# An encoder's bidirectional recurrence on one core: the identity of the last two doubling levels added by GpSimd, and the inputs of the carried states multiplied 128 wide

## The reference

```
def _rwkv7_step(S, inp):
    r, w, k, v, a, b = inp
    Sa = jnp.einsum('zbhvk,zbhk->zbhv', S, a)
    S = S * w[..., None, :] + Sa[..., :, None] * b[..., None, :] + v[..., :, None] * k[..., None, :]
    return S, jnp.einsum('zbhvk,zbhk->zbhv', S, r)
...
    xs = (shared(r), per_dir(decay), per_dir(kd), shared(v), -kk_s, kk_s * per_dir(a))
    S0 = jnp.zeros((2, B, H, N, N), f32)
    _, ys = lax.scan(_rwkv7_step, S0, xs)
    y = jnp.moveaxis(ys[:, 0] + jnp.flip(ys[:, 1], axis=0), 0, 1)
```

## Time and profile before

| | us |
|---|---|
| median of 3 runs | 1809.4 (1805.44 to 1811.64) |
| the profiled execution's own time | 1806.69 |
| its span in the profile | 1804.9 |
| recurrence, eight passes | 368.9 to 590.0 of the span |
| TensorE busy | 1709.2 (95%) |
| VectorE busy | 556.7 (31%) |
| ScalarE busy | 334.5 (19%) |
| GpSimd busy | 71.3 (4%) |

### The profile page before, as it was taken

The page is one execution under the profiler, slowest core; times in us unless marked ns, Lnnn a source line. Parts: engine busy times, 40 slices in busy tenths (PEclk is TensorE's granted clock), DMA queues, the critical chain, the costliest instruction groups (busy, mean ns, idle before and its releaser), DMA issues.

```text
span 1804.9 us, 36910 instructions
## 1 busy us (share of the span) xinstructions
PE 1709.2 (95%) x15975; PEld 1092.5 (61%) x15975; DVE 556.7 (31%) x1270; ACT 334.5 (19%) x966; POOL 71.3 (4%) x114
## 2 busy tenths in 40 slices
PE   8999999989999999999999999999999999999996
PEld 7887888877777445576554545454444444454543
DVE  2001333577875101023123232222223222322233
ACT  2122222156656101022100000000000000000002
POOL 1000000010100000002000000000000000000000
PEclk9999999999999999999999999999999999999998
DMA  9932344200000925247999999999999999999994
GB/s 303 216 112 97 117 136 171 93 4 4 4 4 5 366 100 193 105 175 269 398 388 427 433 425 434 427 434 428 432 429 431 428 432 428 432 430 426 413 423 191
DMA packets 100784, 503.61 MB, mean 279 GB/s; under 512 B 38204, under 2 KB 42704, under 8 KB 81472
## 3 DMA queue, kind: packets, MB, share of 16 engines
q1 hardware_dynamic: 95960, 489.22, 67.7%
q0 software_dynamic: 4464, 12.03, 2.3%
q10 hardware_dynamic: 248, 0.65, 0.1%
HBM read 511.29 MB, written 4.23 MB: 286 GB/s over the span
## 4 chain that ended last, share of the span: by engine, by line
PE 73%; DMA 20%; DVE 4%; issue 2%; SPq 1%; ACT 1%; POOL 0%; DVEq 0%; ACTq 0%; PEldq 0%
PE ps L1598 15%; DMA ring<-in_wd 9%; PE ps L2120 9%; DMA ring<-in_wu 9%; PE ps L2112 8%; PE ps L2263 8%; PE ps L1930 6%; PE ps L2128 4%; PE ps L1813 2%; PE ps L1948 2%; PE ps L1999 2%; PE ps L2016 2%; PE ps L1957 2%; DMA ring<-in_wg 1%; PE ps L1816 1%
## 5 line engine op out<-in xcount | busy, mean ns | idle before, releaser
L1598 PE MATMUL ps<-wide,ring 128*128 128x256 f32 x1248 | 275.3, 379 | 1.2 <-PE ps L1598 0.9
L1598 PEld LDWEIGHTS ps<-wide,ring 128*128 128x128 f32 x1248 | 239.0, 195 | 39.7 <-issue 10.1
L2120 PE MATMUL ps<-ring,wide 128*64 128x256 f32 x1472 | 172.0, 394 | 24.1 <-DMA ring<-in_wu 24.1
L1458 DVE TENSOR_TENSOR tokA<-tokA,ps 128x512 f32<-128x512 f32 x256 | 158.5, 681 | 105.0 <-PE ps L2128 105.0
L2112 PE MATMUL ps<-ring,wide 128*64 128x256 f32 x1600 | 180.5, 383 | 4.4 <-DMA ring<-in_wg 2.4
L2263 PE MATMUL ps<-ring,gg 128*64 128x512 f32 x736 | 168.1, 598 | 2.8 <-DMA ring<-in_wd 2.8
L2120 PEld LDWEIGHTS ps<-ring,wide 128*64 128x64 f32 x1472 | 109.6, 142 | 84.8 <-DMA ring<-in_wu 28.5
L1471 DVE SCALAR_TENSOR_TENSOR gg<-ps,tmp,gg 128x256 f32<-128x256 f32 x32 | 15.5, 484 | 471.0 <-PE ps L2120 471.0
L2112 PEld LDWEIGHTS ps<-ring,wide 128*64 128x64 f32 x1600 | 114.4, 138 | 62.6 <-issue 4.3
L2128 PE MATMUL ps<-wide,gg 64*128 64x512 f32 x512 | 135.3, 627 | 0.6 <-ACT wide L889 0.6
L2263 PEld LDWEIGHTS ps<-ring,gg 128*64 128x64 f32 x736 | 48.7, 136 | 116.8 <-issue 106.1
(11 more groups left out here) (361 smaller groups left out, 1994.8 us busy)
## 6 DMA issues: line engine op xcount, KB each, us to landing
ring<-in_wu SPq DMA_DIRECT2D x20, 4096.0 KB, 29.0
ring<-in_wg SPq DMA_DIRECT2D x19, 4096.0 KB, 29.6
ring<-in_wd SPq DMA_DIRECT2D x19, 4096.0 KB, 30.4
rest<-in_wd SPq DMA_DIRECT2D x8, 4096.0 KB
ring<-in_w_in SPq DMA_DIRECT2D x7, 4096.0 KB, 15.9
rest<-in_wg SPq DMA_DIRECT2D x6, 4096.0 KB
rest<-in_wu SPq DMA_DIRECT2D x6, 4096.0 KB
ring<-in_w_out SPq DMA_DIRECT2D x4, 4096.0 KB, 17.6
```

Of the source, the lines that this page charges most:

```text
L1458: V.tensor_tensor(fin_part(t, h, n), fin_part(t, h, n), ps[:, banks[q][h], :], ALU.add).then_inc(S["added"], 1)
L1598: ins = mm(ps[0:rows_, m % 2, 0:T], lhs, hnT[:, k, :], start=k == 0, stop=k == KD - 1)
L2120: ins = mm(ps[CAP * h:CAP * h + CAP, 1, 0:T], xT[:, k, CAP * i:CAP * i + CAP], w[:, T * h:T * h + T], start=k == 0, stop=k == KD - 1)
```

## The change

In levels 4 and 5 the identity is added to the power by GpSimd, into a new tile `PI`, so that one product (P + I)·R takes the place of P·R + R. The step then waits for GpSimd and no longer for ScalarE directly. `rw_r1` and `rw_ks` become one counter `rw_plus`, which GpSimd raises 14 times in a pass. The input products of the states are taken for both heads at once: 64 rows of weights, 128 columns, 128 wide moving data. The two off-diagonal blocks of the result are not used. `SS` becomes 128 wide, and ScalarE copies 128 columns in place of 64.

```
-        SS = late[:, 5120:5376].rearrange("p (z i n) -> p z i n", z=2, i=2)
+        PI = late[:, 5888:6400].rearrange("p (g e n) -> p g e n", g=4, e=2)
+        SS = late[:, 5120:5632].rearrange("p (z i n) -> p z i n", z=2, i=2)
...
             for n in range(4 * CT):
                 pool.wait_ge(S["rw_mask"], n + 1)
-                pool.tensor_tensor(PRN[1][:, n % 4, :, 1, :], GB[:, n % 4, :, 0, :], eye, ALU.add).then_inc(S["rw_r1"], 1)
+                pool.tensor_tensor(PRN[1][:, n % 4, :, 1, :], GB[:, n % 4, :, 0, :], eye, ALU.add).then_inc(S["rw_plus"], 1)
                 if n % 4 == 3:
                     for b in range(TB):
-                        pool.tensor_tensor(KS[:, b], GK[:, b, :, 1, :], GK[:, 2 + b, :, 1, :], ALU.add).then_inc(S["rw_ks"], 1)
+                        pool.tensor_tensor(KS[:, b], GK[:, b, :, 1, :], GK[:, 2 + b, :, 1, :], ALU.add).then_inc(S["rw_plus"], 1)
+                    for i in range(8):
+                        pool.wait_ge(S["rw_pte"], 23 * (n // 4) + 12 + i)
+                        pool.tensor_tensor(PI[:, i % 4], PRN[i // 4][:, i % 4, :, 2, :], eye, ALU.add).then_inc(S["rw_plus"], 1)
...
-                        A(SS[:, z, i % 2, :], ps[:, S_BANK[i % 2] + 2 * z, T:T + CH], ACT.Copy).then_inc(S["rw_se"], 1)
+                        A(SS[:, z, i % 2, :], ps[:, S_BANK[i % 2] + 2 * z, T:T + P], ACT.Copy).then_inc(S["rw_se"], 1)
...
                     if n == 11:
                         pe.wait_ge(S["rw_pv"], p + 1)
+                    elif l >= 4:
+                        pe.wait_ge(S["rw_plus"], 14 * p + 6 + n - 15)
                     else:
                         pe.wait_ge(S["rw_pte"], 23 * p + (n - 3 if n < 11 else n - 4))
...
-                    lo = 0 if l < 4 else 1
-                    for e, r, q, o in tiles():
-                        mm(ps[o, 2 * g + e, CH * lo:P], src[q, g, e, 2, :], src[q, g, e, lo:2, :].rearrange("p k n -> p (k n)"),
-                           start=True, stop=False)
-                    for e, r, q, o in tiles():
-                        ins = mm(ps[o, 2 * g + e, CH:P], ident[q, q], src[q, g, e, 1, :], start=False, stop=True)
+                    if l < 4:
+                        for e, r, q, o in tiles():
+                            mm(ps[o, 2 * g + e, 0:P], src[q, g, e, 2, :], src[q, g, e, 0:2, :].rearrange("p k n -> p (k n)"),
+                               start=True, stop=False)
+                        for e, r, q, o in tiles():
+                            ins = mm(ps[o, 2 * g + e, CH:P], ident[q, q], src[q, g, e, 1, :], start=False, stop=True)
+                    else:
+                        for e, r, q, o in tiles():
+                            ins = mm(ps[o, 2 * g + e, CH:P], PI[q, g, e, :], src[q, g, e, 1, :], start=True, stop=True)
...
-                        for e in range(2):
-                            mm(ps[half_of(e), S_BANK[i % 2] + 2 * z, T:T + CH], NB[q, g, P + CH * e:P + CH * e + CH], X[q, g, 0, e, :],
-                               start=True, stop=False)
-                        for e in range(2):
-                            ins = mm(ps[half_of(e), S_BANK[i % 2] + 2 * z, T:T + CH], NB[q, g, T + CH * e:T + CH * e + CH], value(q, g % 2, e),
-                                     start=False, stop=i == 0)
+                        heads = ps[:, S_BANK[i % 2] + 2 * z, T:T + P]
+                        mm(heads, NB[q, g, P:T], X[q, g, 0].rearrange("p e n -> p (e n)"), start=True, stop=False)
+                        ins = mm(heads, NB[q, g, T:T + P], Vtok[q, g % 2, P * p:P * p + P], start=False, stop=i == 0)
```

More of the change, by code:

```diff
@@ L271, in encoder @@
         ya_tr ya_ev rw_sq rw_n2 rw_bonus_in rw_bon rw_q rw_exp rw_prep rw_n2e rw_y0e rw_gram rw_mask rw_gnow rw_v0 rw_sums rw_pv rw_kv rw_x0
-        rw_x0ev rw_pt rw_pte rw_rh rw_tte rw_r1 rw_xf rw_xe rw_ks rw_y0 rw_s rw_se rw_ys rw_yp
+        rw_x0ev rw_pt rw_pte rw_rh rw_tte rw_plus rw_xf rw_xe rw_y0 rw_s rw_se rw_ys rw_yp
         rw_mu rw_dsq rw_var rw_out op_mm op_add xk_mm xk_ev xs_mm xs_max xs_exp xs_p xs_tr xs_trev xo_mm xo_ev
@@ L1855, in pair_ @@
                                 mm(ps[half_of(e), 2 * b + h, T:T + CH], X[q, g, 0, e, :], GB[q, g, e, 1, :], start=z == 0, stop=False)
-                    pe.wait_ge(S["rw_ks"], 2 * p + b + 1)
+                    pe.wait_ge(S["rw_plus"], 14 * p + 4 + b + 1)
                     for h in range(2):
@@ L1886, in carried @@
                         q = half_of(e)
-                        ins = mm(ps[q, S_BANK[i % 2] + 2 * z, T:T + CH], TT[q, g, :], SS[q, z, (i - 1) % 2, :], start=False, stop=True)
+                        n = slice(CH * e, CH * e + CH)
+                        ins = mm(ps[q, S_BANK[i % 2] + 2 * z, T + CH * e:T + CH * e + CH], TT[q, g, :], SS[q, z, (i - 1) % 2, n], start=False, stop=True)
                     ins.then_inc(S["rw_s"], 1)
@@ L1893, in outputs @@
                         q = half_of(e)
-                        ins = mm(ps[q, 5 + 2 * z, T + CH * c:T + CH * c + CH], SS[q, z, i % 2, :], RH[q, g, CH * h:CH * h + CH],
+                        ins = mm(ps[q, 5 + 2 * z, T + CH * c:T + CH * c + CH], SS[q, z, i % 2, CH * e:CH * e + CH], RH[q, g, CH * h:CH * h + CH],
                                  start=True, stop=True)
```

2 lines of the change are left out of this document (1 added, 1 removed).

## The result

| | changed kernel | kernel before |
|---|---|---|
| median, us | 1809.4 (1805.35 to 1814.97, 20 runs) | 1806.54 (1803.29 to 1811.64, 20 runs) |
| ratio, 95% interval | 1.0016 [1.0009, 1.0023] | |
| profiled execution: own time, span | 1809.79, 1808.0 | 1806.69, 1804.9 |

Both columns come from the same chip, in turns. The change costs 2.9 us, 0.16%: no change by the bound of 0.3%, but more than nothing by the interval. The two profiled executions are 3.1 us apart.

The account below looks back on a forecast made before the run. TensorE was taken to bound the doubling levels, with some idle waits for instructions. Terms -0.93 + 1.40 - 0.75 + 0.67 gave +0.39 us a pass, 3.1 in eight; forecast 1812 us, range 1803 to 1821.

Parts of the forecast that it names:

- (a): Levels 4 and 5: eight steps lose their four identity products, 0.93 us less a pass on TensorE's path.
- (c): Instruction waits in the doubling levels: 176 of 1783 instructions fewer a pass, 0.75 us less, ends 0 and 1.15.
- (b): Levels 4 and 5: TensorE waits for GpSimd's additions, 1.40 us more a pass, ends 1.2 and 2.0.
- (d): Input products and state copies: wider products and copies lengthen the carried chain by 0.67 us a pass, ends 0.4 and 1.0.
- level 5's wait: Step 17 to step 22's transposes: 0.50 us later although five removed groups (0.58) lie between, so the wait is 1.08.
- Level 4's 0.32: Step 16 can start only after step 12's eviction and GpSimd's addition, 0.32 us later a pass.
- the pattern of all: Recurrence: the fifth pass, 26.70 us, was read as typical of all eight because its instruction counts are the same.
- The 0.12 that I had let come back: First input products: of 0.42 us lengthening, about 0.12 returns as the second step no longer waits and restarts the pipeline.
- A: Levels: instruction queue is the real bound and hides GpSimd waits; 5.4 us less than before, 1803; chance 0.2.
- B: Levels, decisively step 17 to 22: GpSimd's additions wait for VectorE; 16 us more, 1825; chance 0.15.
- C: Input products: their widening is hidden by ScalarE's copies and costs nothing; -2 us, 1806; chance 0.1.

Follow-up runs that it names:

- e4: Kernel before with the identity left out of levels 4 and 5, so a different inverse, and no GpSimd wait: 1796.75 us, ratio 0.9942 to the kernel before.
- e1: Changed kernel's levels with the old input products, copies and 64-wide states: 1801.35 us, ratio 0.9977 to the kernel before.
- e2: Changed kernel's input products and states with the old levels: 1813.59 us, ratio 1.0036 to the kernel before.
- e7: Changed kernel with 128 weight columns but only head 0's 64 moving columns in the input products: 1807.88 us, ratio 1.0011 to the kernel before.
- e8: Kernel before, with GpSimd making its eight identity additions a pass that no product reads: 1805.84 us, ratio 0.9997 to the kernel before.
- e10: e1 with one more GpSimd addition of the same size ahead of each of level 5's four: 1826.26 us, ratio 1.0125 to the kernel before.
- e6: Kernel before with GpSimd adding the identity in level 4 only, squarings ahead of the wait: 1800.05 us, ratio 0.9970 to the kernel before.
- e11: e6 with level 3's identity also added by GpSimd, its 128-wide product split in two: 1799.38 us, ratio 0.9971 to the kernel before.
- e3: e1 with eight one-column products replacing the identity's eight in each step of levels 4 and 5: 1809.77 us, ratio 1.0021 to the kernel before.
- e9: Changed kernel with 64 weight and 128 moving columns, four input products per chunk: 1805.80 us, ratio 1.0004 to the kernel before.

## Why the prediction was right, and which terms were not

Forecast 1812 (1803 to 1821), measured 1809.4, and the forecast of the difference, 3.1 us, met 2.9. The 2.6 us between the numbers are the base: the three runs shown had a median of 1809.4, twenty have 1806.5, near the profiled execution's own 1806.7. The mechanisms are those of the forecast, but that the sum fits this well is luck: two terms were each too large, with opposite signs. Per pass, us:

| term | forecast | measured | from |
|---|---|---|---|
| (a) + (c), removed products and instruction waits | -1.68 | -1.22 | e4, 9.8 / 8 |
| (b), wait for GpSimd | +1.40 | +0.58 | e1 less e4, 4.6 / 8 |
| the levels together | -0.28 | -0.65 alone, -0.40 in the changed kernel | e1, 5.2 / 8; table, 3.23 / 8 |
| (d), input products and copies | +0.67 | +0.89, +0.80 | e2, 7.1 / 8; table, 6.37 / 8 |
| sum | +0.39 | +0.36 | 2.9 / 8 |

**(a)** was counted from the row of the identity groups. The array's work did fall by that, but not the way: on the stretch from step 17 to step 22 the five groups gave 0.19 us in place of 0.58 (e4), since ScalarE's evictions end the next wait. It wasn't measured apart from (c).

**(b)** The term that was mis-sized most: 1.40 forecast, 0.58 measured. What failed is the pricing of the two waits as if nothing else stood in their place. The distances themselves were right. In the changed kernel's fifth pass step 17's transposes end at 500.62, and steps 21, 22 and the transposes of 22 start 1.24, 1.79 and 2.07 us later; the working had 1.31, 1.76 and 1.99. But of the 1.08 booked as level 5's wait, 0.39 is ScalarE's, which e4 has without GpSimd; the working had booked the same 0.39 as gain in (a). Against e4 level 5's wait is 0.66 a pass. And in the kernel before, three passes waited for instructions on just this stretch (2.83 to 2.85 us in place of 1.93), so there the later additions cost nothing more. Level 4's 0.32 came in one pass of eight, the fifth, which the working was read from: step 16's squaring is 0.44 us further behind step 15's there than before (0.72 for 0.28) and starts 0.05 behind the addition. It is the only pass of the changed kernel without a wait for instructions of over 0.25 us in its levels. In the others such a wait stands ahead of step 16, and the squaring is at most 0.06 further behind step 15's. So the fifth pass was not the pattern of all.

**(c)** I took 0.75, with the issue waits down from 9.2 to about 3. In e1 they are 2.7, in the changed kernel 6.5, in e4 4.4. (a) and (c) together show 0.29 us a pass for (c) if (a) is 0.93, and 0.68 if (a) is the 0.54 that the ways were shortened by; the second is an estimate from e4's stretch above, near the 0.75. Which instruction a block of instructions ends at shifts with every edit ahead of it, and so does what it meets. So single profiles are a poor measure of this term, and its size apart from (a) rests on that estimate.

**(d)** Both stages had the right mechanism: the halves overlap (first to first carried is 1.34, not 1.7), and the copies show 277 ns for the 0.27 expected. The first stage grew by 0.40 us instead of 0.30. The 0.12 that I had let come back from the second step did not: the groups of the changed kernel, two rounds of 0.11 each, follow by 0.23 to 0.33 us. The second stage grew by 0.34, forecast 0.32 (the change of tile shape shows 0.21 there for the 0.11, the longer rounds the rest), and the last by 0.055, forecast 0.05. That the round is long because the moving side is 128 wide was right only in part: 128 columns of weights do the same (e7).

**The rivals.** A, faster by 5.4 us: its mechanism is at work in the levels, as (b) shows, and e1 is 5.2 us faster; but the inputs part takes it back, and the issue waits did not vanish. B, the additions at 0.52 us and more: they show 507 ns in the changed kernel, and 445 in e8, where nobody waits for them. Its mechanism is there, at less than its size. In the changed kernel the 51 additions of an identity beside a VectorE operation with two SBUF inputs average 530 ns (up to 696), and 11 with no VectorE operation beside them 410. VectorE's operations are held up as well, as in this row of the kernel's timeline (alone such an operation takes 420 ns, beside an addition 538 in the mean):

```profile
501.43 0.66 DVE L1088 TENSOR_TENSOR tokA<-tokA 128x256 f32<-128x256 f32 x1
```

The Trainium skill's "GPSIMD Engine Reference", "Specifications", names contention on the SBUF interfaces when VectorE has two SBUF inputs, and the trace agrees. In the first and the last pass, where level 5's additions take 0.41 us, the way from step 17 to step 22 is 2.32 us, in the other six 2.50 to 2.84. Of the place B was right too: e10 doubles GpSimd's work there and pays for all of it. C, the wide products hidden: excluded by e2.

**The best version** of those run is e6, with e11 level with it: 1800.05 us, 0.9970 of the kernel before, 9 us under the changed kernel. It keeps the half of the edit whose additions are ready in time.

## What to carry to other kernels

Work moved to an idle engine costs nothing as work (e8). It costs its handover and its duration at the places where the result is wanted next: here one level had a whole level's time ahead of it and paid next to nothing, the next had two steps and paid all that was won. Price each place by itself, against what would be waited for there without the move, and try the edit at each alone. Merging small products into a wider one halves the instructions and not the array's time: when the array is the bound and quarters were already running side by side, the unused blocks of the wide product are paid for.

## What the runs showed of the hardware

**Waits for instructions come at fixed counts.** In each of the fourteen traces I counted TensorE's records, its sequencer's among them, and looked in the recurrence for small products without a semaphore that TensorE's sequencer takes up more than 0.25 us behind the one before. There are 22 before, 12 in the changed kernel, 10 in e1, 13 in e6 and 21 in e8. All of them stand where the running count leaves a remainder of 193 or 194 when divided by 256, and none elsewhere:

```
kernel before, start of the gap (us) : length (us) : count mod 256
383.1 : 0.86 : 193      386.2 : 1.41 : 193      390.5 : 0.87 : 193
414.4 : 1.55 : 194      418.8 : 0.88 : 194      442.6 : 1.20 : 193
```

I read them as waits for the next 256 instructions where the last ones passed too fast. The DMA records bear this out. All 191 gaps of the fourteen traces end 1.2 to 2.0 us (median 1.4) behind the end of a packet of 16384 bytes on the instruction queue. The ends of two gaps are never less than 3.45 us apart, so in this stage TensorE got 256 instructions per 3.45 us at best. The changed kernel's page has 91 packets on the instruction queue, where it was 96. Its fifth pass still has 7:

```profile
q8 instruction: 91, 1.49, 0.3%
```

The Trainium skill, "Runtime: NRT & Kernel Launch", "Instruction fetch mechanics", gives the block of 256, which agrees. It calls the cost of crossing into the next one "mostly hidden", which 9.2 us of issue waits in this recurrence do not.

**A one-column product is not cheap.** Eight records of one moving column hold the quarters for 0.09 us, eight of 64 columns for 0.117 (e3).

**The wider side sets the round.** A round of small fp32 records takes 0.058 us with 64 columns of weights and of moving data, and 0.11 with 128 of either (e7, e9).

**GpSimd and VectorE lengthen each other.** An addition of 128 by 128 took 410 ns alone and 530 in the mean beside a VectorE operation with two SBUF inputs. That operation took 420 alone and 538 beside an addition (changed kernel).
